# Three K units of the last four gate column groups computed as 2x2 blocks in seven products

## What is computed

```python
h = rms_norm(x, norm_mix)
(qa, ka, va, ..., gc, gates) = split_cols(h @ w_in, IN_SPLITS)   # gates: 3 * 2048 columns
y_a = swa_attention(...)      # eight heads
y_b = stick_breaking(...)     # four heads
y_c = nsa_attention(...)
g_a, g_b, g_c = jnp.split(gates, 3, axis=-1)
merged = (sigmoid(g_a) * (y_a @ w_br_a)
          + sigmoid(g_b) * (y_b @ w_br_b)
          + sigmoid(g_c) * (y_c @ w_br_c))
x = x + merged @ w_out
x = x + (silu(h2 @ w_gate) * (h2 @ w_up)) @ w_down;  out = rms_norm(x)
```

## Time and profile before

| | |
|---|---|
| median of 3 runs | 1354.35 us (1353.66 to 1357.03) |
| profiled execution, its own time | 1354.56 us |
| its span, first to last instruction | 1352.8 us |
| time outside the span | 1.76 us |
| PE busy | 1343.6 us, 99% |
| DVE busy | 1016.8 us, 75% |
| ACT busy | 729.9 us, 54% |
| POOL busy | 46.6 us, 3% |
| mean granted TensorE clock | 0.998 |

### The profile page before, as it was taken

The page is one execution under the profiler, slowest core; times in us unless marked ns, Lnnn a source line. Parts: engine busy times, 40 slices in busy tenths (PEclk is TensorE's granted clock), DMA queues, the critical chain, the costliest instruction groups (busy, mean ns, idle before and its releaser), DMA issues.

```text
span 1352.8 us, 26568 instructions
## 1 busy us (share of the span) xinstructions
PE 1343.6 (99%) x11202; PEld 1308.9 (97%) x11202; DVE 1016.8 (75%) x1380; ACT 729.9 (54%) x958; POOL 46.6 (3%) x70
## 2 busy tenths in 40 slices
PE   9999999999999999999999999999999999999997
PEld 8888999999999999999999999999999999999997
DVE  6454557667644766767899999889897899988984
ACT  7333356656545664456655555555454555555554
POOL 4000000000000110000000000000000000000003
PEclk9999999999999999999999999999999999999999
DMA  7767555444565667555566666665666666666563
GB/s 261 249 224 222 182 171 157 152 141 141 156 187 171 188 195 229 185 188 168 184 208 204 213 195 192 195 203 181 210 211 202 194 215 191 193 196 232 191 204 139
DMA packets 135265, 261.08 MB, mean 193 GB/s; under 512 B 8448, under 2 KB 25408, under 8 KB 134768
## 3 DMA queue, kind: packets, MB, share of 16 engines
q1 hardware_dynamic: 132944, 251.14, 58.3%
q0 software_dynamic: 1792, 7.57, 1.6%
q10 hardware_dynamic: 416, 0.75, 0.2%
HBM read 257.33 MB, written 2.10 MB: 192 GB/s over the span
## 4 chain that ended last, share of the span: by engine, by line
PE 99%; DMA 0%; ACT 0%; DVE 0%; issue 0%; DVEq 0%
PE bank L686 22%; PE bank L688 22%; PE bank L687 22%; PE bank L928 9%; PE bank L925 9%; PE bank L927 9%; PE bank L674 3%; PE bank L824 1%; PE bank L735 1%; DMA x<-in_x 0%; PE bank L784 0%; PE bank L1071 0%; PE bank L736 0%; PE bank L872 0%; PE bank L850 0%; PE bank L864 0%
## 5 line engine op out<-in xcount | busy, mean ns | idle before, releaser
L1412 DVE TENSOR_TENSOR weight_lo_ring<-raw_ring,weight_hi_ring 128x1024 fp32r<-128x1024 f32 (+2 forms) x479 | 580.5, 1216 | 242.3 <-ACT weight_hi_ring L1134 185.6
L1134 ACT ACTIVATE weight_hi_ring<-raw_ring 128x1024 fp32r<-128x1024 f32 (+2 forms) x431 | 449.8, 1049 | 421.6 <-PE bank L688 206.2
L686 PE MATMUL bank<-weight_hi_ring,hT_hi 128*128 128x256 f32 (+2 forms) x1276 | 380.9, 298 | 0.0
L687 PE MATMUL bank<-weight_lo_ring,hT_hi 128*128 128x256 f32 (+2 forms) x1276 | 375.5, 294 | 0.0
L688 PE MATMUL bank<-weight_hi_ring,hT_lo 128*128 128x256 f32 (+2 forms) x1276 | 375.5, 294 | 0.0
L686 PEld LDWEIGHTS bank<-weight_hi_ring,hT_hi 128*128 128x128 f32 x1276 | 239.8, 188 | 10.0 <-issue 3.4
L687 PEld LDWEIGHTS bank<-weight_lo_ring,hT_hi 128*128 128x128 f32 x1276 | 239.9, 188 | 6.1
L688 PEld LDWEIGHTS bank<-weight_hi_ring,hT_lo 128*128 128x128 f32 x1276 | 239.7, 188 | 6.3
L686 PE MATMUL bank<-weight_hi_ring,h2T_hi 128*128 128x256 f32 x704 | 195.2, 277 | 0.0
L687 PE MATMUL bank<-weight_lo_ring,h2T_hi 128*128 128x256 f32 x704 | 194.4, 276 | 0.0
L688 PE MATMUL bank<-weight_hi_ring,h2T_lo 128*128 128x256 f32 x704 | 194.4, 276 | 0.0
(11 more groups left out here) (292 smaller groups left out, 2457.7 us busy)
## 6 DMA issues: line engine op xcount, KB each, us to landing
raw_ring<-in_w_in SPq DMA_DIRECT2D x96, 512.0 KB, 3.4
raw_ring<-in_w_gate SPq DMA_DIRECT2D x88, 512.0 KB, 4.3
raw_ring<-in_w_up SPq DMA_DIRECT2D x88, 512.0 KB, 4.0
raw_ring<-in_w_down SPq DMA_DIRECT2D x88, 512.0 KB, 4.4
raw_ring<-in_w_in SPq DMA_DIRECT2D x55, 480.0 KB, 4.3
raw_ring<-in_w_out SPq DMA_DIRECT2D x32, 512.0 KB, 3.9
raw_ring<-in_w_br_c SPq DMA_DIRECT2D x16, 256.0 KB, 3.9
raw_ring<-in_w_br_a SPq DMA_DIRECT2D x16, 256.0 KB, 7.2
```

The lines of the kernel that those rows point to most:

```text
L686: pe.matmul(dst, x_hi, w_hi, start=opening, stop=False, skip_group_check=True)
L687: pe.matmul(dst, x_hi, w_lo, start=False, stop=False, skip_group_check=True)
L1134: act.activation(whi[:, s, :, 0:width(u)], raw[:, s, :, 0:width(u)], ACT.Copy)\
L1412: dve.tensor_tensor(lo, w, hi.bitcast(F32), ALU.subtract).then_inc(lo_ready, 1)
```

## The change

Slots 73, 74, 75 (gate 8), 83, 84, 85 (gate 9), 93, 94, 95 (gate 10) and 103, 104, 105 (gate 11) go through `block_unit` with seven products. The other five units of these groups go through it too, with eight products, in another order of the same 24 matmuls, because the two banks now hold other quarters of the result.

- PE: products 1 and 6, 4 and 7 are summed in the other pair of banks. The first such unit waits until the group before has been emptied; the next group waits for `gate_products_folded`.
- DVE: sums of the weights and their `lo` for each of the twelve units; sums of `hT` once, at slots 61, 64 and 67; `fold_gate` after the third such unit; and `finish_gate` after the group, which writes the whole gate sum to `sigmoid_gates`.
- ACT: `hi` of the sums for each unit; `copy_gate_products` after the third; and the sigmoid, now in place on `sigmoid_gates`, two slots later than before.
- The loads from HBM are the same.

```diff
+GATE_SEVEN = (3, 4, 5)
+GATES_BY_SEVENS = (8, 9, 10, 11)
+GATE_SUMS_SLOT = 61
 def evac_engine(q):
-    return "act" if CHUNKS[q][0] == "gate" else "dve"
+    return "act" if CHUNKS[q][0] == "gate" and not gate_by_sevens(q) else "dve"
...
+            def gate_unit(u, lhs, q, j):
+                pe.wait_ge(lo_ready, u + 1)
+                sums = None
+                if is_seven(u):
+                    n = GATE_SEVEN.index(j)
+                    if gates_folded(q) == 1:
+                        pe.wait_ge(hT_sum_lo, n + 1)
+                    if n == 0:
+                        pe.wait_ge(emptied[evac_engine(q - 1)], evac_count(q - 1))
+                    sums = (hS[n][:, 0, :, :], hS[n][:, 1, :, :])
+                pair, other = 2 * (q % 2), 2 * (1 - q % 2)
+                block_unit(u, ("gate", q), lhs, UK * j, sums, pair, pair + 1, j == UPC - 1, six=other).then_inc(unit_used, 1)
             def straight(u):
                 if j == 0:
                     pair_free(q)
+                    if gate_by_sevens(q - 1):
+                        pe.wait_ge(gate_folded, gates_folded(q - 1))
...
+            def copy_gate_products(v, q):
+                i = CHUNKS[q][1]
+                act.wait_ge(unit_used, v + 1)
+                act.wait_ge(emptied["dve"], evac_count(branch_q[i - SIG]))
+                quarter = sig[:, i % SIG, :, :].rearrange("p t (c n) -> p (t c) n", c=2)
+                act.activation(quarter[:, 0:4:3, :], bank[2 * (1 - q % 2)][:, :].rearrange("p (q c) -> p q c", q=2),
+                               ACT.Copy).then_inc(gate_copied, 1)
...
-                if j == n - 1 and kind == "gate":
+                if v in GATE_MID:
+                    copy_gate_products(v, GATE_MID[v])
...
+                if v - 2 in CHUNK_OF:
+                    p, jp = CHUNK_OF[v - 2]
+                    if gate_by_sevens(p) and jp == UPC - 1:
+                        act.wait_ge(emptied["dve"], evac_count(p))
+                        for t in range(TT):
+                            tile = sig[:, CHUNKS[p][1] % SIG, t, :]
+                            last = act.activation(tile, tile, ACT.Sigmoid, scale=rstd[:, t:t + 1])
+                        last.then_inc(emptied["act"], 1)
+                if j == n - 1 and kind == "gate" and not gate_by_sevens(q):
...
+            def fold_gate(v, q):
+                seven = bank[2 * (1 - q % 2) + 1][:, :].rearrange("p (q c) -> p q c", q=2)
+                quarter = gate_quarters(q)
+                dve.wait_ge(unit_used, v + 1)
+                dve.wait_ge(gate_copied, gates_folded(q))
+                chain(dve.tensor_tensor(gate_u_two[:, :], quarter[:, 0, :], quarter[:, 3, :], ALU.add))
+                chain(dve.tensor_tensor(quarter[:, 1:3, :], seven, gate_u_two[:, :].unsqueeze(1).to_broadcast([P, 2, Q4]),
+                                        ALU.add))
+                dve.tensor_tensor(quarter[:, 3, :], seven[:, 0, :], quarter[:, 2, :], ALU.add).then_inc(gate_folded, 1)
+            def finish_gate(v, q):
+                quarter = gate_quarters(q)
+                two, three = (bank[2 * (q % 2) + b][:, :].rearrange("p (q c) -> p q c", q=2) for b in range(2))
+                dve.wait_ge(unit_used, v + 1)
+                dve.wait_ge(gate_folded, gates_folded(q))
+                dve.tensor_tensor(quarter[:, 1:3, :], two, quarter[:, 1:3, :], ALU.add)
+                dve.tensor_tensor(quarter[:, 0:4:3, :], three, quarter[:, 0:4:3, :], ALU.add).then_inc(emptied["dve"], 1)
```

More of the change, by code:

```diff
@@ L128, with gate_by_sevens @@
 LAST_BANK = 6
+CHUNK_OF = {}
+for _q, (_k, _i, _u, _n) in enumerate(CHUNKS):
+    for _j in range(_n):
+        CHUNK_OF[_u + _j] = (_q, _j)
+def gate_by_sevens(q):
+    return q < Q_FFN and CHUNKS[q][0] == "gate" and CHUNKS[q][1] in GATES_BY_SEVENS
 def by_sevens(h, c):
@@ L141, in is_seven @@
 def is_seven(u):
+    if U_MIX <= u < U_OUT:
+        q, j = CHUNK_OF[u]
+        return gate_by_sevens(q) and j in GATE_SEVEN
     if not U_FFN <= u < U_END:
@@ L226, in evac_engine, with gates_folded @@
 def evac_engine(q):
-    return "act" if CHUNKS[q][0] == "gate" else "dve"
+    return "act" if CHUNKS[q][0] == "gate" and not gate_by_sevens(q) else "dve"
+def gates_folded(q):
+    return sum(gate_by_sevens(p) for p in range(q + 1))
 def evac_count(q):
@@ L699, in pair_free, with into @@
                 if q >= 2:
-                    how = evac_engine(q - 2)
-                    pe.wait_ge(emptied[how], evac_count(q - 2))
+                    pe.wait_ge(emptied[evac_engine(q - 2)], evac_count(q - 2))
+            opened = set()
+            def into(i, b, q, lhs, rhs, stop):
+                l_hi, l_lo = lhs
+                r_hi, r_lo = rhs
+                dst = bank[b][:, q * Q4:(q + 1) * Q4]
+                pe.matmul(dst, l_hi, r_hi, start=(i, b) not in opened, stop=False, skip_group_check=True)
+                opened.add((i, b))
+                pe.matmul(dst, l_hi, r_lo, start=False, stop=False, skip_group_check=True)
+                return pe.matmul(dst, l_lo, r_hi, start=False, stop=stop, skip_group_check=True)
@@ new lines, in quarters, with block_unit, block, total @@
+            def quarters(u, k, c):
+                return tuple(m[:, u % RING, k, c * Q4:(c + 1) * Q4] for m in (whi, wlo))
+            def block_unit(u, key, lhs, k0, sums, two, three, stop, six=6):
+                def block(k, t):
+                    return tuple(m[:, k0 + k, t * P:(t + 1) * P] for m in lhs)
+                if not is_seven(u):
+                    for k in range(UK):
+                        into(key, three, 0, block(k, 0), quarters(u, k, 0), stop)
+                        into(key, two, 0, block(k, 0), quarters(u, k, 1), stop)
+                        into(key, two, 1, block(k, 1), quarters(u, k, 0), stop)
+                        m = into(key, three, 1, block(k, 1), quarters(u, k, 1), stop)
+                    return m
+                def total(r):
+                    return tuple(m[:, r, :] for m in sums)
+                def extra(r):
+                    return tuple(m[:, r, :] for m in ext_buffer(u))
+                into(key, six, 0, block(0, 0), quarters(u, 0, 0), True)
+                into(key, three, 0, block(1, 0), quarters(u, 1, 0), stop)
+                into(key, two, 0, total(3), quarters(u, 1, 1), stop)
+                into(key, six, 1, total(1), quarters(u, 0, 1), True)
+                pe.wait_ge(ext_ready, N_SEVEN[u] + 1)
+                into(key, six + 1, 0, total(0), extra(0), True)
+                into(key, six + 1, 1, total(2), extra(1), True)
+                return into(key, two, 1, block(1, 1), extra(2), stop)
```

112 lines of the change are left out of this document (66 added, 46 removed).

## The result

The changed kernel takes 1367.84 us, the median of 6 runs (1365.87 to 1371.0); the kernel before takes 1354.34 us beside it. The ratio is 1.0094 (95% interval 1.0081 to 1.0107): 0.9% slower. The forecast was 1361.8 us with a range from 1356.0 to 1366.5.

What follows compares the result with a forecast made beforehand. PE was taken to bound the kernel, busy 1343.6 of 1352.8 us. Minus 4.1 gained plus 11.6 of stalls gave a span of 1360.3 and a forecast of 1361.8 us, range 1356.0 to 1366.5.

Steps and rivals of the forecast that it cites:

- the lead of the first `lo`: Time the run's first `lo` ends before PE needs it; below 4.9 us, PE stands still at the third unit.
- Gain: Gates 8 to 11: 36 matmuls fewer at 0.1133 us each save 4.08 us, 0.30%.
- What PE would wait for: DVE's `lo` at each third unit, at most 2.5 us; slots 85 to 88, 93 for head 2's mask, 95, 104, 105, 108.
- The round: DVE and ACT taking turns on one seven-product unit: 4.84 us in all, against PE's 2.38 us.
- Sums of `hT` at nothing: Slots 61, 64 and 67: costed at nothing because DVE waits there, or 0.7 us each without that cover.
- Gate 9's lead: Slot 83's `lo` ends at 439.9, 3.5 us before PE comes at 443.4; stall 1.4 us at slot 85.
- Gates 10 and 11: Stalls of 3.7 us in each of the two gates, plus 0.8 us at slot 108.
- the 0.8 us: Slot 108: its load is issued some 7 us later, PE comes 6 later; 0.8 us of wait taken, 0 to 4.5 possible.
- The clock: PE's granted clock in the changed gates: expected to stay at 1.00, the 2.4 GHz level.
- The amount of DVE's work: DVE gets 10.5 us more per gate, making 29.3 and 30.6 us in stretches of 30 in gates 9 and 10.
- The sign that DVE would have almost no idle time: Slots 80 to 105: DVE almost never idle would show the forecast right.
- Table load: ACT, gates 9 and 10: each load costs 1.28 us; rival that it costs double, 1374.4 us, chance 0.02.

Runs made afterwards that it cites:

- the mixed kernel: Two sum buffers, sigmoids behind the last head, seven-product units 2, 3, 4 in gates 8, 9, 3, 4 in 10, 4 in 11, against the kernel before: 1353.78 us.
- The two-buffer kernel: The changed kernel with a second buffer for the sums of the weights, so DVE makes the next unit's sums ahead of this unit's `lo`: 1358.19 us.
- the fastest version: Kernel before plus two sum buffers, seven-product units 2, 3, 4 in gates 8, 9, 3, 4 in 10, 4 in 11, sigmoids two slots after each gate: 1352.63 us.
- Late sigmoids: The changed kernel with the sigmoids of gates 8 to 11 moved to slots 111 to 113, behind the last head: 1366.48 us.

## Why the prediction was right in direction and wrong in size

The median is 6.0 us above the forecast. Of these, 4.0 stand in the profiled execution: 1.0 in gate 8, 2.1 in gate 9, 0.9 in gate 10 and 0.1 between the gates, against terms of 0.1, 3.3, 3.7 and 0. The step that failed is the lead of the first `lo` in gates 8 and 9, put at 4.9 and 3.5 us. It was 4.2 and 2.6, since the sums of `hT` were costed at nothing, the round was 0.16 us too short, and gate 8's lateness reached gate 9. In gate 10 the clock, put at 1.00, took 1.7 us that no term had, and the wait at slot 95 gave most of it back. The other 2.0 us lie between the profiled execution and the median (the forecast had 0.2 the other way), and their cause stays open. Measured again, the same kernel took 1366.14 us, so how far the time lies beyond the range is less than two measurements of it differ.

- **Gain.** 36 x 0.1133 = 4.08 us. Right; the spacing of the matmuls in gates 8 to 11 at full clock is unchanged, and in the mixed kernel 27 fewer matmuls brought slot 108 forward by 3.2 us against 3.06.
- **What PE would wait for.** Right: the third unit of each run, slots 85 to 88, head 2's mask, 95, 104, 105, the longest 2.5 us. The two-buffer kernel shows that the taking of turns causes half of these waits; the rest is argued.
- **The round.** The term was 4.84 us and measured 5.00: the three sums take 1.62 us (411.31 to 412.93) where I had 1.53, and the gaps between the instructions sum to 0.23 us where I had 0.16. My 1.53 ended where the next instruction starts, and on DVE that is some 0.1 us before the one ahead ends, while ACT waits for the end. That the FFN's round is 5.00 as well is chance, since another unit's `lo` is in it. The error is 0.3 us for each run of three that waits.
- **Sums of `hT` at nothing.** This failed, and it is 0.6 of gate 8's 1.0 us. The cover was there for the sums but not for the last `lo`, 0.68 us at 404.67, which stood ahead of slot 73's sums when DVE no longer had room. Moving them took the wait at slot 75 from 1.00 to 0.40. I had named 0.7 us as its price without cover, and it belonged in the sum. With the round's 0.3 us that is the whole of gate 8: a lead of 4.2 us, and 2 x 5.00 - 2 x 2.38 - 4.2 = 1.0.
- **Gate 9's lead.** I had the `lo` of slot 83 at 439.9 with a lead of 3.5. It ended at 441.45 while PE came at 444.06, a lead of 2.6, and slots 84 and 85 waited 2.8 us in place of 1.4. Of the 1.55 us, 0.55 were there at slot 73's `lo` and 0.3 came from gate 8's two rounds. Another 0.43 came through the ring, which the forecast had only at slot 108: SP issued the load of slot 79 when the `lo` of slot 75 was written, at 420.37, and ACT stood for it.

```profile
425.47 2.13 ACT L1198 ACTIVATE weight_hi_ring<-raw_ring 128x1024 fp32r<-128x1024 f32 x2 [1.77 <-DMA raw_ring<-in_w_br_c]
```

DVE then stood 0.43 us for this `hi`, and head 0's abs began at 428.29, where I had it near 427. The rest, some 0.3 us, goes with the sums of slot 83, which took 1.40 us beside POOL. These parts are my estimate from the rows. Moving the sums of `hT` helped gate 9 by 0.2 us only, since PE came earlier as well. The lead is most of 5.4 in place of 3.3.
- **Gates 10 and 11.** Forecast 3.7 and 4.5 (with slot 108), measured 4.6 and 4.5. In gate 10 the mask's wait of 1.9 us came as forecast (1.93). Slot 108 had no wait of its own: the 0.8 us was wrong, and gate 11's rounds took what it gave, 1.80 and 2.53 for 1.3 and 2.5. That the two errors cancel is luck.
- **The clock.** This step was missing, and in the profiled execution it is 1.7 of gate 10's 4.6 us. I read 1.00 in a kernel in which PE never stood, and carried it over to one in which it stands ten times. A wait of some 2 us can be followed by some 3.5 us at 1.2 GHz, at 1.7 us each. It came once in the first profile and twice in the second, where other waits shrank by nearly as much; in the second, gate 10 lost 4.2 us with its clock up, so the clock explains about half of gate 10's excess. It does not explain why the median lies above the profiled execution: the longest of the first six, 1371.0 us, has the same mean granted clock as the profiled one, 0.998, and the shortest, 1365.87, has 0.996. The Trainium skill has it (page "TensorE: Matmul & The Clock Gate", section "Part 1: The HAM clock gate"): the clock follows how busy PE has been lately. The traces agree in that it fell only behind waits; they do not show which wait is followed. I had read it for what the change adds, and not for what its waits would bring.
- **The amount of DVE's work.** I used it as support, "29 to 31 us of 30". Wrong: measured it is 29.1 of 35.4 in gate 9's stage, and 26.8 of 30.0 in the fastest version, which has three such units in this stage too, at 2, 3 and 4, and no wait. The 10.5 us for each gate were right in sum (1016.8 to 1062.2 us is 45.4, for 42 and the sums of `hT`), but they do not fall evenly: 7.2 us more in gate 9's stage, 12.0 in gate 11's. And I set them against stretches that were not whole stages. The sign that DVE would have almost no idle time was wrong too: 6.3 us of gate 9's stage were idle.
- **Table load.** Nothing behind 1.28 us in the changed kernel either: the loads at 428.84 and 430.67 are followed by their activations at 430.13 and 431.97. Late sigmoids have four table loads fewer, and that brought nothing measurable. So the drain that the prediction quotes from the Trainium skill (page "ScalarE: Activation LUTs", section "What ACT_TABLE_LOAD costs") does not show here.
- **Range.** The unknowns in it were those that I had named. It left out the one with no row in the kernel before, the clock, and nearly all the small errors had one sign, since a delay lengthens the next; only slot 108's had the other.

## What to carry to other kernels

Before a chain of one engine is spread over two, write down one round of it, who waits for whom, and compare the round with the consumer's time for the same piece: with one buffer between them the round is the sum of both engines' parts, with two it is the longer one. Even then, fewer of the costly pieces, placed where the lead is long, were the only versions here that came out below the kernel before, by 2.1 us. And when a change makes an engine wait that never waited, its clock of before is no row to go by.
